# Attention in a hybrid encoder on one core: gate sums as two fp32r matmuls, probabilities scaled in place and transposed

## The reference

```
proj = h @ w_in
q, k, v, f_logit = jnp.split(proj, [D, 2 * D, 3 * D], axis=-1)
log_f = jax.nn.log_sigmoid((f_logit + b_f).astype(jnp.float32)).transpose(0, 2, 1)
cum = jnp.cumsum(log_f, axis=-1)
# per block of 128 queries:
logits = einsum('bhqd,bhkd->bhqk', q_i, k) * hd ** -0.5 + c_i[..., :, None] - cum[..., None, :]
logits = jnp.where(kpos[None, :] <= qpos[:, None], logits, -jnp.inf)
p = jax.nn.softmax(logits, axis=-1)
o = einsum('bhqk,bhkd->bhqd', p, v)
return o @ w_out
```

## Time and profile before

| what | value |
| --- | --- |
| median of 3 runs | 3188.09 us |
| the profiled execution | 3189.45 us |
| its span | 3187.7 us |
| TensorE busy | 2888.0 us (91%) |
| VectorE busy | 1970.8 us (62%) |
| ScalarE busy | 1474.7 us (46%) |
| mean granted TensorE clock | 0.948 |
| DMA, mean | 197 GB/s |

### The profile page before, as it was taken

How to read it: one execution, slowest core, us unless ns; L and a number is a source line. 1 busy time by engine, 2 the same in 40 slices (tenths; PEclk the granted TensorE clock), 3 DMA queues, 4 the chain that set the end, 5 groups by cost and what they waited for, 6 DMA issues and landing times.

```text
span 3187.7 us, 63222 instructions
## 1 busy us (share of the span) xinstructions
PE 2888.0 (91%) x24254; PEld 2598.9 (82%) x24254; DVE 1970.8 (62%) x2557; ACT 1474.7 (46%) x2011; POOL 136.2 (4%) x160
## 2 busy tenths in 40 slices
PE   2399999899999999985999798989789999999998
PEld 2399999888888899984888677767687888889998
DVE  6877777876666666678564344444337666665434
ACT  0133333466666643348554232322236666665333
POOL 0000000100000000000000221211000000000000
PEclk8599989999999999997999899999799999999999
DMA  8787877756666578872655454444444666655553
GB/s 297 259 279 266 290 262 264 268 170 192 188 191 188 185 241 290 274 238 69 189 178 178 136 172 142 151 159 160 128 144 152 185 186 185 188 184 175 183 172 126
DMA packets 506155, 628.09 MB, mean 197 GB/s; under 512 B 26392, under 2 KB 434824, under 8 KB 505736
## 3 DMA queue, kind: packets, MB, share of 16 engines
q1 hardware_dynamic: 501952, 622.62, 60.6%
q10 hardware_dynamic: 4040, 3.07, 0.3%
HBM read 623.50 MB, written 2.10 MB: 196 GB/s over the span
## 4 chain that ended last, share of the span: by engine, by line
PE 76%; DVE 10%; DMA 7%; ACT 3%; issue 3%; ACTq 0%; DVEq 0%; SPq 0%
PE ps L1799 26%; PE ps L1783 21%; PE ps L1802 13%; PE ps L1979 9%; DMA raw<-in_ffn_w_out 4%; DVE macc L1182 3%; DVE wlo L1161 2%; PE ps L2028 2%; ACT whi L752 1%; PE ps L1825 1%; PE ps L1816 1%; DMA raw<-in_mod_w 1%; DVE mx L1490 1%; PE ps L1889 1%; DMA raw<-in_fox_w_in 1%
## 5 line engine op out<-in xcount | busy, mean ns | idle before, releaser
L1161 DVE TENSOR_TENSOR wlo<-raw,whi 128x1024 fp32r<-128x1024 f32 x792 | 966.6, 1228 | 721.5 <-ACT whi L752 720.5
L752 ACT ACTIVATE whi<-raw 128x1024 fp32r<-128x1024 f32 x792 | 833.0, 1059 | 939.2 <-PE ps L1802 312.9
L1799 PE MATMUL ps<-xs,whi 128*128 128x512 f32 x3328 | 1172.1, 397 | 18.7 <-DVE xs L1245 10.9
L1802 PE MATMUL ps<-xs,wlo 128*128 128x256 f32 x3328 | 935.5, 281 | 0.0
L1799 PEld LDWEIGHTS ps<-xs,whi 128*128 128x128 f32 x3328 | 627.4, 189 | 168.1 <-issue 11.6
L1783 PE MATMUL ps<-act,whi 128*128 128x256 f32 x3840 | 708.5, 287 | 38.6 <-DVE wlo L1161 38.2
L1783 PEld LDWEIGHTS ps<-act,whi 128*128 128x128 f32 x3840 | 608.3, 195 | 45.7 <-DVE wlo L1161 44.9
L1802 PEld LDWEIGHTS ps<-xs,wlo 128*128 128x128 f32 x3328 | 631.9, 190 | 0.0
L1783 PE MATMUL ps<-act,wlo 128*128 128x256 f32 x1920 | 548.7, 286 | 0.0
L1783 PEld LDWEIGHTS ps<-act,wlo 128*128 128x128 f32 x1920 | 374.2, 195 | 0.0
L1182 DVE SCALAR_TENSOR_TENSOR macc<-raw,cact,macc 128x1024 f32<-128x1024 f32 (+1 forms) x252 | 293.0, 1163 | 9.0 <-DMA raw<-in_mod_w 4.2
(11 more groups left out here) (258 smaller groups left out, 3052.8 us busy)
## 6 DMA issues: line engine op xcount, KB each, us to landing
raw<-in_ffn_w_in SPq DMA_DIRECT2D x352, 512.0 KB, 3.6
raw<-in_mod_w SPq DMA_DIRECT2D x288, 512.0 KB, 5.1
raw<-in_ffn_w_out SPq DMA_DIRECT2D x176, 512.0 KB, 4.7
raw<-in_fox_w_in SPq DMA_DIRECT2D x96, 512.0 KB, 5.6
raw<-in_mod_w SPq DMA_DIRECT2D x128, 384.0 KB, 4.9
raw<-in_fox_w_out SPq DMA_DIRECT2D x32, 512.0 KB, 7.2
raw<-in_rwkv_w_r SPq DMA_DIRECT2D x32, 512.0 KB, 4.2
raw<-in_rwkv_w_k SPq DMA_DIRECT2D x32, 512.0 KB, 4.1
```

The lines of the kernel that those rows point to most:

```text
L752: sc.activation(whi[:, half, :, :].rearrange("p k n -> p (k n)"), slots[slot], ACT.Copy).then_inc(w_hi, 1)
L1161: v.tensor_tensor(wlo[:, half, :, :].rearrange("p k n -> p (k n)"), slots[slot], whi[:, half, :, :].rearrange("p k n -> p (k n)").bitcast( ...
L1799: pe.matmul(ps[bank + m][:, :], whi[:, half, k, m * P:m * P + P], src[:, kt, :, :].rearrange("p u s -> p (u s)"), start=kt == 0, stop=Fals ...
L1802: last = pe.matmul(ps[bank + m][:, 0:S], wlo[:, half, k, m * P:m * P + P], src[:, kt, 0, :], start=False, stop=kt == KT - 1, skip_group_ch ...
```

## The change

The negative sums `negc` are split once, in lap 0, into an fp32r part `neghi` and the rest `neglo` (two more VectorE instructions; a third one makes `oner`, the ones as fp32r). `select` writes both parts, four instructions instead of two, into an `nsel` of type fp32r. In the scores the fp32 matmul with ones becomes two fp32r matmuls, one for each part. For the probabilities VectorE no longer builds `diag` but multiplies `ex` in place with the reciprocals, and TensorE turns it with plain transposes (`pe.transpose`). No instruction changes its place relative to the slabs.

```diff
-        nsel = take(r, "nsel", [HEADS, 2, S])
+        neghi = take(r, "neghi", [HEADS, S], F32R)
+        neglo = take(r, "neglo", [HEADS, S])
+        nsel = take(r, "nsel", [HEADS, 2, 2, S], F32R)
+        oner = take(r, "oner", [HEADS, P], F32R)
...
-        diag = take(r, "diag", [P, 2, 2, P])
...
+            v.tensor_copy(oner[:, :], ones[0:HEADS, :]).then_inc(*fg_v.inc("one"))
             v.wait_ge(*fg_a.at("hi"))
             v.tensor_tensor(wfl[:, :, :], wf[:, :, :], wfh[:, :, :].bitcast(F32), ALU.subtract).then_inc(*fg_v.inc("lo"))
...
+                v.wait_ge(*fg_v.at("neg"))
+                v.tensor_copy(neghi[:, :], negc[:, :]).then_inc(*fg_v.inc("nhi"))
+                v.wait_ge(*fg_v.at("nhi"))
+                v.tensor_tensor(neglo[:, :], negc[:, :], neghi[:, :].bitcast(F32), ALU.subtract).then_inc(
+                    *fg_v.inc("nlo"))
...
                 for h in range(2):
-                    v.tensor_scalar(nsel[:, h, :], negc[:, :], con[0:HEADS, ds(a_ * 2 + (K_ID + h), 1)], None,
-                                    ALU.mult).then_inc(*at_v.inc(f"sel{h}"))
+                    for u, src in enumerate((neghi[:, :].bitcast(F32), neglo[:, :])):
+                        v.tensor_scalar(nsel[:, h, u, :], src, con[0:HEADS, ds(a_ * 2 + (K_ID + h), 1)], None,
+                                        ALU.mult).then_inc(*at_v.inc(f"sel{h}{u}"))
...
                     for t in range(2):
-                        v.tensor_scalar(diag[:, h, t, :], ident, dinv[:, h, t:t + 1], None,
-                                        ALU.mult).then_inc(*at_v.inc(f"d{h}{t}"))
+                        part = ex[:, h, 0:P] if t == 0 else ex[:, h, P:3 * P]
+                        v.tensor_scalar(part, part, dinv[:, h, t:t + 1], None, ALU.mult).then_inc(
+                            *at_v.inc(f"d{h}{t}"))
...
-                        last = pe.matmul(dst, ones[0:HEADS, :], nsel[:, h, 0:n], start=False, stop=True,
-                                         skip_group_check=True)
+                        for u in range(2):
+                            last = pe.matmul(dst, oner[:, :], nsel[:, h, u, 0:n], start=False, stop=u == 1,
+                                             skip_group_check=True)
...
                 for h in range(2):
                     for b in range(3):
-                        last = pe.matmul(ps[5 + h][:, b * P:b * P + P], ex[:, h, b * P:b * P + P],
-                                         diag[:, h, min(b, 1), :], start=True, stop=True, skip_group_check=True)
+                        last = pe.transpose(ps[5 + h][:, b * P:b * P + P], ex[:, h, b * P:b * P + P], ident)
```

More of the change, by code:

```diff
@@ L425, in trunk @@
         fg_a = steps("fg_a", "hi e l")
-        fg_v = steps("fg_v", "lo z abs min ls neg")
+        fg_v = steps("fg_v", "one lo z abs min ls neg nhi nlo")
         fx_a = steps("fx_a", "q k v")
         at_pe = steps("at_pe", "s t o")
-        at_v = steps("at_v", "sel0 sel1 sm0 sm1 m00 m01 m10 m11 rd d00 d01 d10 d11 p0 p1 lo0 lo1")
+        at_v = steps("at_v", "sel00 sel01 sel10 sel11 sm0 sm1 m00 m01 m10 m11 rd d00 d01 d10 d11 p0 p1 lo0 lo1")
         at_a = steps("at_a", "e00 e01 e10 e11 hi0 hi1")
@@ L1391, in fox_body @@
                     pieces(ph_fox, i, {5: gate_first, 7: gate_second})
-                    v.wait_ge(*fg_v.at("neg"))
+                    v.wait_ge(*fg_v.at("nlo"))
                 else:
@@ L1881, in scores @@
                 pe.wait_ge(*fx_a.at("k", a_))
-                pe.wait_ge(*at_v.at("sel1", a_))
+                pe.wait_ge(*fg_v.at("one"))
+                pe.wait_ge(*at_v.at("sel11", a_))
                 for h in range(2):
```

## The result

In 20 runs each, the changed kernel took 3164.01 us in the median (3153.24 to 3174.54) and the kernel before 3179.91 (3173.19 to 3192.75). The ratio is 0.9946, 95% interval 0.9932 to 0.9960: by it the kernel is 17 us faster, between 13 and 22. The direction is as forecast; the time lies 1 us under the stated range (3165 to 3187). The profiled execution took 3160.19 us, 29.3 us less than that of before.

The account below looks back on a forecast made before the run. TensorE was taken to fix each attention lap, VectorE and DMA near behind. Gate sums −3.4, probabilities −5.4, VectorE +1.0, low clock on the gate sums −1.0, one fall fewer −3.4: −12.2 us, so 3176 us, range 3165 to 3187.

Parts of the forecast that it names:

- the start of the sum: Time the savings were taken from: 3188.09 us, median of the runs; the profiled execution took 3189.45 us.
- the clock term D: TensorE's clock in the attention laps: one fall fewer, −3.4 us; called the softest term, ends +17 and −24.
- The gate sums (A): Scores: second fp32 matmul of each group becomes two one-pass fp32r matmuls, −0.42 us a lap, eight times: −3.4 us.
- eight changes of K: Scores: K switching between 128 and 16, weight load not hidden, 0.21 us each; eight before and after, so this stays.
- The probabilities (B): Probabilities: twelve fp32 passes become six transposes, −0.67 us a lap, eight times: −5.4 us.
- side estimate: Scores: with the skill's 81 ns spacing, 128-column pairs would save 0.05 us more each, 0.8 us over the kernel.
- Rival 2: Short fp32r is slow in the gate sums, which then save about 0: 3184 us; chance 0.20.
- VectorE (C): VectorE's scaling and doubled select cost 0 per lap; splitting negc in lap 0 costs +1.0 us, once.
- rival 3: Absorbed: probabilities come earlier, but the DMA's last weight pieces set the lap: 3188 us; chance 0.08.
- a sign of being wrong: Forecast wrong if full-speed laps stay at 42.8 us or the number of falls moves by more than two.
- the factor on A: Low clock in the scores makes the gate sums cost 1.29 times as much before: −1.0 us more.
- Rival 1: The clock mostly stays up in the scores: three falls of eight instead of seven, 3167 us; chance 0.20.

Follow-up runs that it names:

- e4: Changed kernel with fp32r ones and gate sums on 128 rows, rows 16 to 127 zero: median 3137.92 us, ratio to the kernel before 0.9889.
- e5: Changed kernel with a lap's four q·k matmuls first, then the eight K = 16 matmuls; scores not the reference's: ratio to the kernel before 0.9869.
- e7: Kernel before with its fp32 ones and gate sums on 128 rows, nothing else changed: ratio to the kernel before 0.9924.
- e3: Kernel before with the one-column matmuls moved from ahead of the scores to behind the q slab: ratio to the kernel before 0.9987.
- e2: Kernel before with only the probabilities changed, gate sums left in fp32: ratio to the kernel before 1.0007.
- e8: Changed kernel on 128 rows with each attention lap's one-column matmuls issued twice: seven laps 299.9 us, one run only.
- e11: Changed kernel once more, unaltered: ratio to the kernel before 0.9967.

## Why the prediction was wrong, and where it was right

The time came out 12 us under the forecast of 3176. Two steps failed, both by size: the start of the sum, which is 8 of the 12 us, and the clock term D, which was too small.

**The gate sums (A)** were sized about right as passes: −0.50 us a lap against −0.42. The part that was set aside as fixed, eight changes of K at 0.2 us, was the larger cost: e4, e5 and e7 show 0.17 to 0.20 us each, 1.3 to 1.6 us a lap, more than A and B together. The change leaves it in. The prediction's side estimate of 0.05 us more for each 128-column pair was counted against the old pair; against the sum's own it is 0.02. It entered nothing.

**The probabilities (B)**: −0.69 us a lap (1.26 to 0.57) against −0.67. Rival 2, a slow short form, is out by A's rows. That transposes had brought the clock up at the start of the program is shown by their pace, 0.20 us and then 0.11; the clock of 1.00 in the earlier trace rows does not show it, as the window of those 0.20 us apart reads 1.00 too:

```profile
33.60:36.80 3.20, 3.20 (x15) 3.20 (x16) 3.20 (x4) 0.00 (x0) 0.00 (x0) 1.00 0.58 126
```

**VectorE (C)**: per lap hidden; the scores of lap 1 start 0.8 us later in the first pair of profiles and 0.1 in the second, for +1.0 expected.

**Absorption**, rival 3, was given 0.08 as an all-or-nothing case and is true in part. Laps at full clock average 42.1 us over eight of them in the two profiles of the changed kernel; the forecast was 41.7 and the single one of before 42.8 (three in e3, with the same instructions, 42.7 to 43.0). So about 0.7 of 1.19 us come through, over seven laps −5.0 us instead of −8.3. Part of the rest is a new wait: over seven laps TensorE stands 0.2 us for VectorE's low parts before, and 0.7 and 3.3 us in the two profiles of the changed kernel. VectorE's own wait for the probabilities fell from 22.1 us to 7.4 in eight passes. What takes the remainder is not shown.

**The clock (D)** failed by its size: "I take one fall fewer: −3.4 us". In both pairs of profiles together, 15 falls in 16 passes became 8 in 16, against a sign of being wrong that stood at a move of more than two in eight. The seven laps took 18.5 us less, of which the passes are 5.0; 13.5 are the clock's. It was 4.4 in the sum (with the factor on A). I saw that lap 5 stood at the border and did not ask how much of the stretch the change takes away: 0.5 of 5.4 us. I also gave every fall one price, 3.4 us; laps with a fall took 1.6 to 5.1 us more than the one without before, and in the changed kernel the falls are not only fewer but cheaper, on average 2.7 us instead of 3.3. Rival 1 (three falls of eight, 3167 us) came nearest, with 0.20 to its name: three in the first profile, five in the second. e2 and e8 show that it goes with the stretch's length: unchanged in e2, the falls stay; lengthened in e8 without other scores, they return.

Over all runs the clock's gain is smaller than in the profiles. Both profiles of before are executions with much low clock: 0.948 and 0.947 on average, where only 8 of 64 runs of that kernel had 0.948 or less. The means over runs are 0.9510 (64) before and 0.9526 (30) in the changed kernel. By them about 10 us of low clock are gone, which at half the pace is an estimate of 5 us at most, give or take 3; in the one set that holds both kernels' clocks (e11's) they differ by less, 0.9512 and 0.9516. So the direction and the cause of D hold; its size is open between about what the sum had and three times as much.

**The start of the sum** is what put the time outside the range. The three runs shown had a median of 3188.09 us. The 20 runs of the result had 3179.91, and later sets of 16 to 29 runs of the same kernel 3177.74 to 3182.55, so the start lay some 8 us above the kernel's usual time. The ratio applied to 3188.09 gives 3171 us, inside the range; the effect alone, −17 us (13 to 22) against −12.2, would not have left it. A range for a time should have held the scatter of such a set.

**Sum by stage**: attention in two pairs of profiles 632.2 to 611.2 us, −21. The runs say −17 (13 to 22) and, in e11's, −10 (4 to 18). That both executions profiled of before lay about 10 us above the medians of their sets (3189 us each) fits the larger number; how much of the difference it explains is not settled, as stages that the change does not touch scatter by 16 us from profile to profile.

## What to carry to other kernels

Read where TensorE's granted clock falls before counting passes. A stretch of thin work between dense ones is worth shortening, splitting or moving as a whole, since a lap with a fall was here 1 to 5 us longer beside what the thin instructions themselves cost. Small matmuls on few rows between matmuls on 128 rows pay at every change; filling the rows with zeros removed it. Putting them together saved time as well, but in the order tried here the scores were wrong. When the two engines of a loop are nearly level, count only a part of what one saves. And take the starting time from as many runs as the result will have: the three runs and the profile here lay 8 to 10 us above the usual.

## What the runs showed of the hardware

- A change between 16 and 128 rows from one matmul to the next costs 0.17 to 0.20 us, in fp32 and in fp32r (e4, e5, e7).
- The longer the thin stretch, the more laps fall: 5.4 us, 19 of 21; 4.9 us, 8 of 21; 4.8 us, 4 of 7; 4.1 us, 4 of 7; 3.7 us, 1 of 7; 3.6 to 3.9 us with the one-column matmuls in it, none of 35. The same instructions fall in one lap and not in the next. The mean clock of the runs goes the same way, from 0.951 before to 0.954 to 0.957 where no lap falls.
- Transposes pass at full clock 0.11 us apart, and no fall came at the probabilities in laps 1 to 7 of any kernel.
- Two fp32r matmuls of 128 columns, each with its own weight load, and a change of K take 0.37 us, only 0.05 us less than the two passes of one fp32 matmul. With 256 columns it is 0.43 us against 0.63.
